# Three of four attention units have their probabilities cut by GpSimd, and one by VectorE

## The reference, cut to what matters

```
sparse   8 heads:  logits over the keys of blocks 0..i for query block i, a mask keeps the best 256
window  16 heads:  logits over blocks i-1..i+1, a slope by distance, a sink added to the sum
latent  16 heads:  logits over all 4 blocks
each:    p = softmax(logits);   out = p @ v
```

## Time and profile before

| | |
|---|---|
| median of 3 runs | 2327.12 us (2324.8 to 2329.89) |
| the profiled execution's own time | 2331.24 us |
| its span | 2329.2 us |
| PE busy | 2177.2 us (93%) |
| DVE busy | 1567.4 us (67%) |
| POOL busy | 1495.4 us (64%) |
| ACT busy | 916.9 us (39%) |
| sparse attention | about 225 to 285 us of the span |
| window attention | about 1710 to 1807 us |
| latent attention | about 2062 to 2207 us |

### The profile page before, as it was taken

The page is one execution under the profiler, slowest core; times in us unless marked ns, Lnnn a source line. Parts: engine busy times, 40 slices in busy tenths (PEclk is TensorE's granted clock), DMA queues, the critical chain, the costliest instruction groups (busy, mean ns, idle before and its releaser), DMA issues. The chain is left out here.

```text
span 2329.2 us, 37477 instructions
## 1 busy us (share of the span) xinstructions
PE 2177.2 (93%) x13120; PEld 1210.9 (52%) x13120; DVE 1567.4 (67%) x2848; ACT 916.9 (39%) x1606; POOL 1495.4 (64%) x1032
## 2 busy tenths in 40 slices
PE   6998898999989999989999999999988989989897
PEld 4543544555546666544555555554555444446544
DVE  6497876998996677038898888953047344566633
ACT  2311511455556666543333333332157123245522
POOL 6785585768755555467777877653854768734473
PEclk9999998999999999999999999998999999989998
DMA  7332643579978999988999999861310223300021
GB/s 280 92 100 92 207 154 118 156 266 351 331 238 267 285 359 341 287 315 315 334 333 314 328 341 329 287 212 48 117 37 1 81 82 91 91 28 1 17 88 41
DMA packets 218058, 451.56 MB, mean 194 GB/s; under 512 B 83200, under 2 KB 132544, under 8 KB 217920
## 3 DMA queue, kind: packets, MB, share of 16 engines
q1 hardware_dynamic: 119696, 313.67, 39.2%
q0 software_dynamic: 27648, 100.68, 12.3%
q10 hardware_dynamic: 70576, 35.40, 6.2%
HBM read 390.86 MB, written 58.82 MB: 193 GB/s over the span
## 5 line engine op out<-in xcount | busy, mean ns | idle before, releaser
L914 PE MATMUL ps<-hT,parts 128*128 128x416 f16 (+1 forms) x4800 | 937.6, 357 | 22.0 <-POOL parts L817 9.5
L914 PEld LDWEIGHTS ps<-hT,parts 128*128 128x128 f16 x4800 | 468.1, 98 | 469.8 <-issue 27.6
L914 PE MATMUL ps<-arena 128*128 128x416 f16 x3072 | 547.5, 341 | 16.9 <-DVE arena L2204 16.1
L914 PEld LDWEIGHTS ps<-arena 128*128 128x128 f16 x3072 | 301.1, 98 | 261.2 <-issue 22.0
L823 POOL TENSOR_TENSOR parts<-ring,parts 128x1024 f16<-128x1024 f32 x120 | 255.9, 2134 | 198.5 <-ACT ring L1564 197.3
L814 POOL TENSOR_SCALAR parts<-ring 128x1024 f16<-128x1024 f32 x141 | 162.6, 1153 | 246.8 <-PE ps L914 210.4
L817 POOL TENSOR_TENSOR parts<-ring,parts 128x1024 f16<-128x1024 f32 x141 | 311.1, 2206 | 11.8
L849 POOL TENSOR_TENSOR arena<-ring,arena 128x1024 f16<-128x1024 f32 x128 | 294.2, 2308 | 23.7 <-ACT arena L1601 21.8
L2199 DVE TENSOR_TENSOR route<-arena 128x416 f32<-128x416 f32 x128 | 183.1, 1430 | 131.7 <-DMA arena<-gate_mem 130.1
L1397 ACT ACTIVATE arena<-ps 128x512 f32<-128x512 f32 (+9 forms) x266 | 135.8, 532 | 241.6 <-PE ps L914 144.7
L914 PE MATMUL ps<-arena,parts 128*128 128x512 f16 x876 | 195.4, 384 | 11.5 <-POOL parts L817 5.8
(11 more groups left out here) (228 smaller groups left out, 2642.7 us busy)
## 6 DMA issues: line engine op xcount, KB each, us to landing
ring<-w SPq DMA_DIRECT2D x133, 512.0 KB, 3.6
ring<-u SPq DMA_DIRECT2D x128, 512.0 KB, 6.2
ring<-v SPq DMA_DIRECT2D x128, 512.0 KB, 4.7
act_mem<-spare SPq DMA_DIRECT2D x128, 208.0 KB, 4.9
gate_mem<-arena ACTq DMA_DIRECT2D x4, 6656.0 KB, 51.3
arena<-act_mem SPq DMA_DIRECT2D x128, 208.0 KB, 4.1
arena<-gate_mem SPq DMA_DIRECT2D x128, 208.0 KB, 5.5
arena<-ada_w SPq DMA_DIRECT2D x48, 512.0 KB, 6.0
```

Of the source, the lines that this page charges most:

```text
L914: ins = [T.matmul(out_, a, b, start=start and j == 0, stop=stop and j == 2) for j, (a, b) in enumerate(((lhs[0], rhs[0]), (lhs[0], rhs[1]) ...
```

## The change

VectorE keeps the low part only of the first unit of each four (u%4 == 0). Units with u%4 of 1, 2 and 3 all take the other way: ScalarE writes a float32 row to a flat buffer, and GpSimd makes high and low from it. The flat buffers are counted by `flat_at` (0, 1, 2 for units 1, 2, 3; 3, 4, 5 for units 5, 6, 7), and still two of them take turns. TensorE waits on `probs_low` before it turns units with u%4 == 2, and no longer before those with u%4 == 0. The weight tile stays behind unit 9 in GpSimd's queue; unit 10 is now behind the tile.

```diff
+        def flat_at(u):
+            return 3 * (u // FOUR) + u % FOUR - 1
         def flat_probsT(un, u):
-            n, w = u // 2 % 2, un["nc"] * P
+            n, w = flat_at(u) % 2, un["nc"] * P
...
             def attention(units, u0, between):
-                for u in range(1, len(units), 2):
-                    n = (u0 + u) // 2
+                for u in range(len(units)):
+                    if u % FOUR == 0:
+                        continue
+                    n = flat_at(u0 + u)
...
-                    if u0 + u >= 2 and u % 2:
+                    if u0 + u >= 2 and u % FOUR != 2:
                         pe.wait_ge(probsT, u0 + u - 1)
                     elif u0 + u >= 2:
-                        pe.wait_ge(probs_low, (u0 + u) // 2)
+                        pe.wait_ge(probs_low, (u0 + u) // FOUR + 1)
...
-                        pe.wait_ge(probs_low, (u0 + u + FOUR) // 2)
-                        pe.wait_ge(flat_cut, (u0 + u + FOUR) // 2)
+                        pe.wait_ge(probs_low, (u0 + u) // FOUR + 1)
+                        pe.wait_ge(flat_cut, 3 * ((u0 + u) // FOUR + 1))
...
-                    if u % 2:
-                        if u0 + u >= 4:
-                            act.wait_ge(flat_cut, (u0 + u) // 2 - 1)
+                    if u % FOUR:
+                        if flat_at(u0 + u) >= 2:
+                            act.wait_ge(flat_cut, flat_at(u0 + u) - 1)
                         own.do(copy(flat_probsT(un, u), turned_row, scale=1.0), probsT)
...
-                    if 3 <= u < len(units) + 3 and u % 2:
+                    if 3 <= u < len(units) + 3 and u % FOUR == 3:
                         low_probs(u - 3)
```

## The result

The changed kernel has a median of 2346.07 us (2339.83 to 2349.81, 5 runs) beside 2326.09 us (2323.84 to 2329.89, 5 runs) of the kernel before. The ratio, taken over all five runs of each, is 1.0078, with a 95% interval of 1.0061 to 1.0095: 18.1 us slower, between 14 and 22. (The two medians alone lie 20.0 us apart.)

What follows compares the result with a forecast made beforehand. It took PE to bound the latent attention, DVE and PE near their limit in the sparse one, and POOL last at `values`. Sparse 10.1, window 2.1 and latent 1.9 made +14.1 us: 2341.2 on the median, range 2328 to 2350.

Steps and rivals of the forecast that it cites:

- The exclusion: Sparse attention: VectorE's L1854 and GpSimd's pairs each wait for the other's whole instruction; with the added pairs, +10.1 us there.
- the clock: Sparse attention: longer TensorE waits may add time at the lower clock; nothing in the sum, up to 4 us in the range.
- The first rival: Latency without the port: GpSimd late only by its own pairs; sparse 3.6 us, total +7.6, 2334.7 us; chance 0.14.
- The chain of units 22 and 23: Sparse attention, third group: unit 23's pair ends at 269.06 instead of 266.27, values start 2.8 us later, 2.5 passes on.
- a stretched L1854 between or beside them: Sparse attention, sign of being right: two 512-wide GpSimd pairs in a row with this, values behind them waiting over 2 us.
- Group by group: Sparse attention's four groups of eight units: +2.9 (with the weight tile), +1.9, +2.5 and +2.8 us, sum 10.1.
- The window attention: Steady state 0, the 0.52 us wait moving to `values`; +1.4 behind the tile, +0.7 at the end; sum 2.1 us.
- The latent attention: Steady state 0, since PE is the bound; +0.95 us behind the tile and +0.95 at the end; sum 1.9.
- What it takes away: At L1807: 40 instructions, some 22 us of DVE, and 40 PE waits go; PE had waited 10.6 us in all.
- Rival two: The slack takes it up: added pairs fall in GpSimd's idle time; +0 to +3 us, 2328; chance 0.13.
- rival three: Faster: DVE bounds the sparse attention and saves, PE gains in the window one; 8.6 us less, 2318.5; chance 0.11.
- ScalarE's output type: ScalarE's copy only changes its output's type; the rows show no price difference, so nothing was taken.

Runs made afterwards that it cites:

- e7: VectorE's sparse-attention products read their second input from PSUM, in two halves, in both kernels: before 0.9989, changed 1.0029; the split costs 3.9 us in that attention.
- e4: Changed kernel plus twelve unused matmuls ahead of the wait of `values` in second halves of the sparse attention: ratio 1.0050 to 1.0086, sparse attention 62.26 us.
- e8: Kernel before plus unused matmuls in its four longest waits at `values`: ratio 1.0001, sparse attention 51.73 us instead of 52.81.
- e3: VectorE's sixteen sparse-attention products cut to 64 of 1024 columns, in both kernels: sparse attention 46.58 us for before, 53.05 for changed.
- e5: The weight tile's three operations go behind units 9, 11 and 13, on both splits; on the kernel before, the sparse attention is 1.6 us longer.

## Why the prediction was right, and where it was off

The forecast was 2341, slower by 14.1 us on its own execution; measured are 18.1 in time and 19.0 in the attentions. The direction and the mechanism came as forecast; the size was some 4 to 5 us short.

- **The mechanism in the sparse attention is shown.** The exclusion was worth 10.1 us (e7), and without it 3.9 us remain. The prediction's own sum for this attention is also 10.1, which is chance: it held 3.6 for plain latency, so only 6.5 for the exclusion, and nothing for the clock that comes with it. The first rival's 3.6 beside the 3.9 is partly chance too, since the 3.9 hold some clock; as a whole that rival (7.6 us more, without the exclusion) falls with e7. The chain of units 22 and 23 was predicted 269.06 - 264.56 = 4.50 us long and measured 4.62, by another order: the second product was expected to wait for unit 22's low part (L866) and to be stretched; it came in ahead of it, unstretched, and the low part took 2.24 us instead. So "a stretched L1854 between or beside them" did not come in this group; GpSimd's stretched rows stand in its place.
- **The term that was mis-sized is the clock.** The prediction put it at nothing in the sum and at up to 4 us in the range. It is 4.5 us of the changed sparse attention (e4), and 1.1 had been lost to it before (e8), so the change added 3.4. With the clock at 1.00 in both kernels the split costs 10.5 us, where the sum had 10.1; with it, 14.0. The 0.94 of the earlier trace rows came from behind the waits of 2.69 and 2.36 us (0.66 from 248 to 253, 0.81 from 278 to 281, 1.00 between). With new waits of 3.5 to 5 us to come, the sum should have had a term for it.
- **Group by group** the sum had 2.9, 1.9, 2.5 and 2.8, and what was added up to each is 1.7, 3.4, 4.1 and 3.7, with 1.0 behind it. The first, with the tile, was too high: more of the lateness lay beside the tile's wait than I took. The second was too low: TensorE comes from the tile without reserve, and I read the excess as the full delay of both wide pairs falling on it, here with unit 14's L864 at 1.51 us and its L866 at 2.24. The groups behind it hold the clock's share.
- **The window attention.** The steady state was right to the digit: 0.52 us at the turn became 0.52 at `values`, and eight units take 11.64 us as before. The tile was 1.4 predicted and about 1.9 measured, the last head 0.7 and 0.1. The products after it at the lower clock, 0.8, were not in the sum. Together 2.9 against 2.1.
- **The latent attention.** 0.95 predicted behind the tile, 0.9 measured; 0.95 at the end, and 0.6 measured, with 0.6 more behind it, where the last products take 1.88 us instead of 1.50 at the lower clock. Together 2.1 against 1.9.
- **What it takes away was worth little, as said.** PE's waits for the low part fell from 10.6 to 3.9 us, more than by half. No attention became shorter for it: the waits at the head of `values` took their place. Rival two (nothing to 3 us more) and rival three (8.6 us less) fall with this.
- **ScalarE's output type** cost nothing that shows: its busy time is 915.1 us against 916.9.

What stays open: why untouched code differs by 11 us in the first stretch from one execution to the next; why a wait of 2.0 us is followed by the lower clock in one execution and not in another; why e3 kept 6.5 us instead of 3 to 4; and how the 10.1 us of e7 and the 4.5 us of e4 overlap. In e7's changed kernel the clock is at 1.00 up to the last 6 us, so the lower clock is mostly a consequence of the exclusion there, and some 7 to 8 us would be pure lateness: 10.5 with both kernels filled, less e7's 3.9 without the 1.1 that its last products took longer at the lower clock (2.45 us, and 1.34 in e4). That split is an estimate, not run. The prediction had 6.5 for it. The losses of the window and the latent attention, some 5 to 6 us, are read from their waits; no run took them apart.

## What to carry to other kernels

Before moving elementwise work between VectorE and GpSimd, look at what else the two read: a single long VectorE product with both inputs in SBUF, here 1.28 us, beside GpSimd's pairs turned a move that cost 3.9 us without the exclusion into one of 14.0. Giving the product one input from PSUM took 10.1 of them back, in an experiment that read an unused bank; no run had the right operand there. Price a wait of TensorE by its length and by the slower products that follow it; where it can't be removed, matmuls that nobody reads kept the clock up here (e4), though in the kernel before they changed no time (e8). And judge such a change by stretches between the same instructions: here one profiled execution showed half of the loss, because untouched code happened to be 9 us shorter. Look at the granted clock of each stretch beside its length, since the same code took up to 2 us more in an attention where the clock had fallen once more.

## What the runs showed of the hardware that was not expected

- Right behind waits of TensorE of 2.04 us (e3) and 3.64 us (after), scores of width 384 took 1.65 us instead of 0.91, and the 10 us from 235 and from 255, with waits of 3.53 and 3.64, had a granted clock of 0.83. With 12 matmuls in the wait it was 1.00 (e4).
- Whether TensorE's clock falls behind a wait of some 2 us is not fixed. At the tile of the window attention it fell behind 2.00 us (before) and not behind 2.01 (e3, before); at the end of the latent one it fell behind 1.90 us (e5, before: the next products took 2.29 us) and not behind 1.90 (before: 1.50).
- A short instruction is kept out by the length of its neighbour: GpSimd's L864 at width 256, from 228.24, took 1.38 us behind the 128x1024 product in the changed kernel, and 0.41 in the same place with the product at 64 columns (e3).
- The product with a PSUM input costs 2 x 748 ns for what two SBUF inputs do in 1280 ns undisturbed, and still the kernel before was no slower with it (0.9989): with their stretching, its sixteen products had taken 23.9 us too.
